# Column sums of the modulation vectors: sixteen or eight small matmuls a section, or a fold on VectorE and one matmul

## The chip, the cores and the metric

One core of one Trainium2 chip. The time is the device time of one execution in microseconds; lower is better. TensorE's clock has two levels, 1.2 and 2.4 GHz, and the profile gives the granted share of the higher one.

## The reference

Two transformer stacks, each of two layers, run one after the other on 256 tokens of width 1024, all in fp32. Each layer has three sublayers: feed-forward, mixer, feed-forward. The first stack also carries 256 context tokens; its mixers are a gated MLP (gMLP) and an attention. The second stack's mixer is a mixture of attention, a causal convolution and gated linear attention. Every sublayer is modulated by vectors that come from a conditioning vector:

```python
def modulation(cond, w_mod, b_mod):
    m = jax.nn.silu(cond) @ w_mod + b_mod
    return jnp.split(m[..., None, :], N_MOD, axis=-1)

def modulate(x, shift, scale):
    return x * (1.0 + scale) + shift
```

A sublayer needs three sections of 1024 values: shift (section 0), scale (1) and gate (2). In the first stack there are two conditions, one for the tokens and one for the context; in the second there is one.

## The kernel before, in words

The twelve sublayers are numbered 0 to 11: 0 to 5 the first stack (feed-forward, gMLP, feed-forward, feed-forward, attention, feed-forward), 6 to 11 the second (feed-forward, mixer, feed-forward, twice). Sublayers 0 to 4 work on two streams (512 tokens), the others on one (256).

All engines' programs are written out by hand. The weights of the large matmuls arrive in units of 1 MB (two loads of 512 KB on SyncE's queue into wraw). For each unit ScalarE rounds them to the high half wh (line 834, split_next), VectorE takes the low half wl = wraw - wh (line 1243, split_next), and TensorE makes three matmuls for each product: high by high, low by high, high by low. wraw, wh and wl have two slots each. In turn i of a loop VectorE first splits the weights of unit i+1, then does what is hosted in that turn, then evacuates unit i (line 1630 in the first stack; in the second stack take, lines 1573 to 1575, stands ahead of the split and product, line 1583, after it). TensorE waits for the split (wlo_done) and for the evacuation of two units before (pair_free). A unit has 48 matmuls: 512 columns wide with two streams (line 2240), 258 or 256 in the second stack (lines 2415, 2439, 2268, 2717). In the second block's mixers the projection's units stand between small steps; the order of VectorE's steps there is fixed: turned queries and keys, kt_t (line 2031), then unit work for the next sublayer's modulation.

The modulation vectors of a sublayer are computed while the sublayer before it runs: that one hosts them. (Sublayer 5's sections 0 and 1 are hosted by the second group of sublayer 3; those of sublayer 6 by loops in sublayer 5.) A section's weights, 1024 x 1024, come in four loads of 1 MB into the two buffers of mraw, and VectorE multiplies them in four units, mod_unit (line 1216), two products of 128x1024 for each condition, into a row of partial sums [128, 1024] (acc or lnp). Tables say in which turn each unit stands (TWO_MODS, NEXT_MODS, FF_MODS, MIX_MODS) and after which unit of TensorE the section is finished (TWO_COLUMNS, NEXT_COLUMNS, FF_COLUMNS). Each mod_unit raises mod_used, on which the load into the buffer that it read waits, in SyncE's queue.

What is left is the sum over the 128 partitions. TensorE does it: for each block of 128 columns one fp32 matmul, with the block of the partial sums as the stationary operand and a column of ones moving, which gives a column of 128 sums in PSUM. columns (line 2129) does 8 in a row in the second stack; column (line 2140) puts 16, one after each group of three, between a unit's matmuls in the first stack's hosts. mod_end (lines 1228 to 1237) copies the columns to modc. In the mixers the sections end with columns after unit 5, after the scores (ahead of unit 10), and after the last output unit; the VectorE steps that belong to them are modulation(4), modulation(8) and modulation(13). After the last, VectorE goes on to arrive, which adds the mixer's output to x (take_chunk, line 1428) and makes the low half of the next sublayer's input (low_chunk, line 1446), for which TensorE waits.

The gates of the first stack (section 2) are summed in another way (ones as the stationary operand, lines 2148 and 2158).

Of the kernel before, what the change touches and what calls it, by code (L numbers as in the profile page):

```python
# [6 lines left out]
P = 128  # L7
B2 = 6
F32 = mybir.dt.float32
F32R = mybir.dt.float32r  # L10
# [169 lines left out]
def program(nc, ins, out, subs):  # L180
    u_end = subs[-1]["n_unit"] + dict(ffn=33, gmlp=36, attn=10, mix=16)[subs[-1]["kind"]]
    with ExitStack() as ctx:
# [44 lines left out]
        pos = sb("pos", [P, TT], I32)  # L227
        cgh_, cgl_ = sb("cgh", [P, KD * 16], F32R), sb("cgl", [P, KD * 16], F32R)
        cgh, cgl = cgh_[:], cgl_[:]


# [91 lines left out]
        bias_full, bias_used = sem("bias_full"), sem("bias_used")  # L323
        cols_ready, mcol_done = sem("cols_ready"), sem("mcol_done")
        gate_ps, gate_row, gate_taken = sem("gate_ps"), sem("gate_row"), sem("gate_taken")
        pair_free = sem("pair_free")
# [112 lines left out]
        def summed(s, sec, c):  # L439

            if s["i"] == 5 and sec in (0, 1):
                return lnp[:, sec]
            return lnp[:, c] if 0 < s["i"] < 5 and sec == 1 else acc[:, c]

        def two(s):
# [744 lines left out]
        def _(dve):  # L1190
# [11 lines left out]
            def mod_unit(s, sec, q):  # L1202
# [9 lines left out]
                for jj in range(2):  # L1212
                    for c in cs:
# [5 lines left out]
                                                      op0=ALU.mult, op1=ALU.add)  # L1219
                    if jj == 1:  # L1220
                        op.then_inc(mod_used, 1)
                    elif q == 0:
                        op.then_inc(bias_used, 1)
                        dve.wait_ge(bias_used, sec + (3 * s["i"] + 2))
                    else:
                        steps.link(op)

            def mod_end(s, sec, bank=4, at=0):

                dve.wait_ge(cols_ready, sec + (sections(s, 0) + 1))  # L1230
                nc_ = len(conds(s))
                dst = modc[:, s["i"] % 2, bass.ds(sec, 1), 0:nc_, :].rearrange("p a c k -> p (a c k)")
                if s["block"] == 2 and isinstance(sec, int) and sec == 2:
# [275 lines left out]
            def rope_tables():  # L1509
# [18 lines left out]
                dve.wait_ge(rope2_ready, 1)  # L1528

            dve.wait_ge(in_full, 3 * 16)  # L1530
            dve.wait_ge(svec_ready, 1)
# [20 lines left out]
            for s in subs:  # L1552
# [329 lines left out]
                elif s["kind"] == "mix":  # L1882
# [10 lines left out]
                    def modulation(i):  # L1893
                        if i == 5:
                            mod_end(nxt, 0, 6, 480)
                        if i == 12:
                            factors(nxt)
                        for sec, q in mix_mods(i):
                            mod_unit(nxt, sec, q)
# [139 lines left out]
                    split_next(u0 + 9)  # L2039
                    mod_end(nxt, 1, 6, 488)  # L2040
                    MP.wait(dve, "scores", turn)
# [77 lines left out]
        def _(pe):  # L2119
            def parts(w_hi, w_lo, x_hi, x_lo):  # L2120

                return (w_hi, x_hi), (w_lo, x_hi), (w_hi, x_lo)

            def columns(s, sec, bank=4, at=0, start=True):

                pe.wait_ge(mod_used, sec * 4 + (12 * s["i"] + 6))
                for c in conds(s):
                    for k in range(KD):
# [4 lines left out]
            def column(s, sec, n, bank=4):  # L2133

                if n == 0:
                    pe.wait_ge(mod_used, sec * 4 + (12 * s["i"] + 6))
                c, k = divmod(n, KD)
                if c >= len(conds(s)):
# [204 lines left out]
            pe.wait_ge(ident_ready, 2)  # L2343
            pe.wait_ge(svec_ready, 1)
            cs = slice(2, 3) if subs[0]["block"] == 2 else slice(0, 2)
            nc_ = len(conds(subs[0]))
# [30 lines left out]
            for s in subs:  # L2377
# [278 lines left out]
                elif s["kind"] == "mix":  # L2656
# [112 lines left out]
                    MA.wait(pe, "decays", turn)  # L2769
                    columns(nxt, 0, 6, 480)  # L2770
                    taps(5)
# [39 lines left out]
                    pe.wait_ge(mcol_done, sections(nxt, 0) + 1)  # L2811
                    columns(nxt, 1, 6, 488)
                    unit(10)
# [92 lines left out]
```

## Time and profile before

| | us |
|---|---|
| median of three runs | 3125.51 |
| lowest, highest | 3121.47, 3126.77 |
| the profiled execution, first to last instruction (its span) | 3123.3 |
| TensorE busy in it | 3058.2 |
| VectorE busy in it | 2027.8 |
| ScalarE busy in it | 969.5 |
| GpSimd busy in it | 673.8 |

The profiled execution has a span and no time of its own outside it. Of the span, what counts is which engine is waited for at each place. In the profile PE is TensorE, PEld its weight load, DVE VectorE, ACT ScalarE, POOL GpSimd, SP SyncE. Matmuls are pipelined, so that durations of neighbours overlap: read the distance between their starts.

### The profile page before, as it was taken

How to read it: one execution, taken by the hardware profiler on the slowest of the kernel's cores; microseconds unless marked ns; L12 is line 12 of the kernel's file. 1: busy time of each engine (PE TensorE's matmuls, PEld its weight loads, DVE VectorE, ACT ScalarE, POOL GpSimd, SP SyncE). 2: the span in 40 equal slices, each digit the busy share in tenths (PEclk: the TensorE clock that was granted, in tenths of full speed). 3: DMA queues.
4: the chain of work that ended last, by engine and by line, in shares of the span. 5: the costliest groups of instructions: out<-in, count | busy, mean ns of one | idle time of the engine just before them, and what ended most of it. 6: DMA issues, size and time to landing. Idle time of an engine off the chain costs nothing.

```text
span 3123.3 us, 46661 instructions
## 1 busy us (share of the span) xinstructions
PE 3058.2 (98%) x19308; PEld 2721.5 (87%) x19308; DVE 2027.8 (65%) x2134; ACT 969.5 (31%) x1027; POOL 673.8 (22%) x614
## 2 busy tenths in 40 slices
PE   8999999999999999999999899999999999999999
PEld 5888889988888888888888699899989999999999
DVE  5854358767278433785638777586788767768754
ACT  2211232212131121221114343333544333344443
POOL 1210100124013010130101022231372313228120
PEclk9999999999999999999999999999999999999999
DMA  7643335332246332463623287586557869755564
GB/s 263 200 150 87 102 102 187 118 101 80 95 131 202 108 90 99 122 202 108 201 99 122 95 268 244 174 266 229 191 174 230 270 193 271 245 189 185 166 182 156
DMA packets 501668, 522.79 MB, mean 167 GB/s; under 512 B 15732, under 2 KB 433830, under 8 KB 501478
## 3 DMA queue, kind: packets, MB, share of 16 engines
q1 hardware_dynamic: 498536, 513.76, 51.5%
q0 software_dynamic: 2944, 6.32, 1.0%
q8 instruction: 143, 2.34, 0.3%
q14 instruction: 45, 0.37, 0.0%
HBM read 518.97 MB, written 1.05 MB: 166 GB/s over the span
## 4 chain that ended last, share of the span: by engine, by line
PE 88%; DVE 7%; ACT 3%; DMA 1%; issue 1%; POOL 0%; SPq 0%; DVEq 0%; ACTq 0%
PE ps L2240 29%; PE ps L2415 16%; PE ps L2326 15%; PE ps L2439 8%; PE ps L2268 8%; PE ps L2305 2%; DVE wl L1243 2%; ACT wh L834 1%; PE ps L2352 1%; PE ps L2284 1%; PE ps L2685 1%; PE ps L2129 1%; PE ps L2717 1%; DVE acc L1216 1%; PE ps L2545 1%
## 5 line engine op out<-in xcount | busy, mean ns | idle before, releaser
L1243 DVE TENSOR_TENSOR wl<-wraw,wh 128x2048 fp32r<-128x2048 f32 x341 | 834.2, 2447 | 569.3 <-ACT wh L834 564.4
L834 ACT ACTIVATE wh<-wraw 128x2048 fp32r<-128x2048 f32 x341 | 652.7, 1914 | 935.7 <-PE ps L2326 383.7
L2240 PE MATMUL ps<-xh,wh 128*128 128x512 f32 (+1 forms) x1504 | 564.9, 376 | 0.5 <-DVE xl L1295 0.3
L2240 PE MATMUL ps<-xl,wh 128*128 128x512 f32 (+1 forms) x1504 | 552.6, 367 | 0.0
L2240 PE MATMUL ps<-xh,wl 128*128 128x512 f32 (+1 forms) x1504 | 550.9, 366 | 0.0
L2415 PE MATMUL ps<-xh,wh 128*128 128x258 f32 x1408 | 405.7, 288 | 5.4 <-DVE xl L1446 3.7
L674 POOL CAST hh<-ht 128x256 f32 (+1 forms) x176 | 140.4, 798 | 1218.1 <-DVE ht L1630 883.3
L2415 PE MATMUL ps<-xh,wl 128*128 128x258 f32 x1408 | 401.2, 285 | 0.0
L2415 PE MATMUL ps<-xl,wh 128*128 128x258 f32 x1408 | 400.7, 285 | 0.0
L1216 DVE SCALAR_TENSOR_TENSOR acc<-mraw,svec,acc 128x1024 f32<-128x1024 f32 x259 | 342.5, 1342 | 5.7 <-DVE prea L1282 0.4
L2240 PEld LDWEIGHTS ps<-xl,wh 128*128 128x128 f32 x1504 | 282.9, 188 | 50.0
L2240 PEld LDWEIGHTS ps<-xh,wl 128*128 128x128 f32 x1504 | 283.4, 188 | 44.8 <-issue 0.7
L2240 PEld LDWEIGHTS ps<-xh,wh 128*128 128x128 f32 x1504 | 283.3, 188 | 44.4 <-issue 1.2
L2415 PEld LDWEIGHTS ps<-xh,wh 128*128 128x128 f32 x1408 | 269.8, 192 | 8.8 <-DVE wl L1243 3.7
L2415 PEld LDWEIGHTS ps<-xl,wh 128*128 128x128 f32 x1408 | 270.6, 192 | 0.0
L2415 PEld LDWEIGHTS ps<-xh,wl 128*128 128x128 f32 x1408 | 270.4, 192 | 0.0
L936 ACT ACTIVATE sg<-ps 128x512 f32<-128x512 f32 (+1 forms) x88 | 48.0, 546 | 660.0 <-PE ps L2240 626.5
L2268 PE MATMUL ps<-wh,xh 128*128 128x256 f32 x832 | 240.6, 289 | 5.1 <-DVE wl L1243 4.9
L2268 PE MATMUL ps<-wl,xh 128*128 128x256 f32 x832 | 234.4, 282 | 0.0
L2268 PE MATMUL ps<-wh,xl 128*128 128x256 f32 x832 | 234.4, 282 | 0.0
L675 POOL TENSOR_TENSOR hl<-ht,hh 128x256 f32 (+1 forms) x176 | 219.9, 1250 | 29.2 <-POOL hh L674 29.2
L2326 PE MATMUL ps<-wh,hh 128*128 128x512 f32 x520 | 205.2, 395 | 1.5 <-DVE wl L1243 1.5
(438 smaller groups left out, 5478.4 us busy)
## 6 DMA issues: line engine op xcount, KB each, us to landing
wraw<-in_ffn_w_in SPq DMA_DIRECT2D x352, 512.0 KB, 5.2
wraw<-in_ffn_w_out SPq DMA_DIRECT2D x176, 512.0 KB, 4.2
mraw<-in_ada_w SPq DMA_DIRECT2D x72, 1024.0 KB, 6.8
mraw<-in_w_mod SPq DMA_DIRECT2D x64, 1024.0 KB, 6.7
wraw<-in_gmlp_w_in SPq DMA_DIRECT2D x48, 512.0 KB, 4.4
wraw<-in_mix_w_in SPq DMA_DIRECT2D x48, 512.0 KB, 4.8
wraw<-in_gmlp_w_out SPq DMA_DIRECT2D x24, 512.0 KB, 3.8
first_w<-in_w_mod SPq DMA_DIRECT2D x8, 1024.0 KB, 11.6
```

Source lines behind the costliest of these rows:

```text
L674: steps.link(pool.tensor_copy(hh[:, where], ht[:, par, 0:width]))
L675: pool.tensor_tensor(hl[:, where], ht[:, par, 0:width], hh[:, where].bitcast(F32), ALU.subtract)\
L834: act.activation(wh[:, slot], wraw[:, slot], ACT.Copy).then_inc(whi_done, 1)
L936: act.activation(sg[:, pair, 0:W], ps[:, 2 * pair, 0:W], ACT.Silu).then_inc(sg_ready, 1)
L1216: op = dve.scalar_tensor_tensor(out=to, in0=mraw[:, q % 2, jj], scalar=svec[:, v, 2 * q + jj:2 * q + jj + 1], in1=biasrow[:] if q == jj == ...
L1243: dve.tensor_tensor(wl[:, slot], wraw[:, slot], wh[:, slot].bitcast(F32), ALU.subtract)\
L2240: m = pe.matmul(ps[:, bank, 0:width], a, b, start=k == p == 0, stop=k == KD - 1 and p == 2)
L2268: m = pe.matmul(to, a, b, start=k == p == 0, stop=k == KD - 1 and p == 2)
L2305: m = pe.matmul(ps[:, 2 * t + half], a, b, start=False, stop=i == kk == 1 and p == 2, skip_group_check=i == 0)
L2326: m = pe.matmul(ps[:, bank0 + 2 * t + half], a, b, start=start and kk == p == 0, stop=stop and kk == 1 and p == 2, skip_group_check=not st ...
L2415: m = pe.matmul(ps[:, 2 * pair + r, 0:XW], a, b, start=n == p == 0, stop=n == KD - 1 and p == 2)
L2439: m = pe.matmul(ps[:, j, 0:T], a, b, start=i == kk == p == 0, stop=i == KF // 2 - 1 and kk == 1 and p == 2, skip_group_check=i == 5)
```

## The change

Where a section is folded (function folded: sections 0 and 1 of sublayers 1 to 5, all three of 7 to 11), VectorE does most of the sum over partitions itself. After the last product it transposes the partial sums in blocks of 32x32, into the buffer of mraw that it has just used up, and sums over each block's 32 columns; this leaves [128, 32], fold, in which each group of 32 partitions holds its part of all 1024 sums. Only then is mod_used raised. TensorE adds the four groups with one fp32 matmul, 32 columns for each condition, whose stationary operand fold_ident is an identity folded to 32 and repeated four times. mod_end picks the sums with four small copies, one for each quarter of the partitions, in place of one.

```diff
+        with ExitStack() as early:
+            fold = early.enter_context(nc.sbuf_tensor("fold", [P, 2, 32], F32))
+        fold_ident = sb("fold_ident", [P, 4, 32])
...
+        def folded(s, sec):
+            return isinstance(sec, int) and (s["i"] in (1, 2, 3, 4, 5) and sec < 2 or s["i"] in (7, 8, 9, 10, 11))
+        def fold_at(s, sec):
+            return sec if s["i"] == 5 else 0
...
-                    if jj == 1:
+                    if jj == 1 and q == 3 and folded(s, sec):
+                        steps.link(op)
+                        for c in cs:
+                            m = steps.mark(dve.transpose(mraw[:, 1, c], summed(s, sec, c)))
+                        for c in cs:
+                            steps.wait(m - len(cs) + 1 + c)
+                            op = dve.reduce_sum(fold[:, c + fold_at(s, sec)], mraw[:, 1, c].rearrange("p (f j) -> p f j", j=32), axis=AX.X)
+                        op.then_inc(mod_used, 1)
+                    elif jj == 1:
                         op.then_inc(mod_used, 1)
...
+                if folded(s, sec):
+                    for b in range(4):
+                        row = slice(32 * b, 32 * b + 32)
+                        dst = modc[row, s["i"] % 2, sec, 0:nc_]
+                        src = ps[row, bank, at:at + 32 * nc_].rearrange("p (c k b) -> p c k b", c=nc_, b=4)[:, :, :, b]
+                        if sec == 2 and s["kind"] == "ffn":
+                            op = dve.tensor_scalar(dst, src, 0.5, None, ALU.mult)
+                        else:
+                            op = dve.tensor_copy(dst, src)
+                    op.then_inc(mcol_done, 1)
+                    return
...
+            dve.wait_ge(ident_ready, 2)
+            steps.link(dve.reduce_sum(fold_ident[:, 0], ident[:].rearrange("p (b i) -> p i b", b=4), axis=AX.X))
+            dve.tensor_copy(fold_ident[:, 1:4], fold_ident[:, 0:1].broadcast_to([P, 3, 32])).then_inc(fold_ready, 1)
...
+            def sums_of_blocks(s, sec, bank, at, start):
+                w, f = 32 * len(conds(s)), fold_at(s, sec)
+                pe.matmul(ps[:, bank, at:at + w], fold_ident[:].rearrange("p b i -> p (b i)"),
+                          fold[:, f:f + len(conds(s))].rearrange("p c f -> p (c f)"), start=start, stop=True,
+                          skip_group_check=not start).then_inc(cols_ready, 1)
...
             def columns(s, sec, bank=4, at=0, start=True):
                 pe.wait_ge(mod_used, sec * 4 + (12 * s["i"] + 6))
+                if folded(s, sec):
+                    sums_of_blocks(s, sec, bank, at, start)
+                    return
...
             def column(s, sec, n, bank=4):
                 if n == 0:
                     pe.wait_ge(mod_used, sec * 4 + (12 * s["i"] + 6))
+                    if folded(s, sec):
+                        sums_of_blocks(s, sec, bank, 0, True)
+                if folded(s, sec):
+                    return
```

fold lies over cgl, which a mixer uses only before its first fold. In the mixers the place of the sums in PSUM moves from columns 480 and 488 of bank 6 to 448 and 480. Before its first matmul TensorE also waits for fold_ready.

## Rows read from the trace of the kernel before

**Rows 1.** The page: busy time and instructions of each engine; chain by engine

```profile
PE 3058.2 (98%) x19308; PEld 2721.5 (87%) x19308; DVE 2027.8 (65%) x2134; ACT 969.5 (31%) x1027; POOL 673.8 (22%) x614
PE 88%; DVE 7%; ACT 3%; DMA 1%; issue 1%; POOL 0%; SPq 0%; DVEq 0%; ACTq 0%
```

**Rows 2.** Lines 2129, 2140: count, ns min/median/max, first and last start, forms

```profile
L2129 PE MATMUL ps<-ones,acc x288: 164/250/353, 1845.1 to 2921.8; 128*128 128x1 f32 x144
...
L2140 PE MATMUL ps<-ones,lnp x160: 164/210/250, 166.4 to 1569.3; 128*128 128x1 f32 x160
...
L2140 PE MATMUL ps<-ones,acc x128: 164/210/250, 129.7 to 1356.2; 128*128 128x1 f32 x128
```

**Rows 3.** Timeline of TensorE, sublayer 5 and mixer: start, us, engine, line, operands, count

```profile
1845.10 1.84 PE L2129 MATMUL ps<-ones,acc 128*128 128x1 f32 x16
1846.81 0.36 PE L2240 MATMUL ps<-xh,wh 128*128 128x256 f32 x1
...
2315.01 0.56 PE L2823 MATMUL ps<-proj,sc_t 128*128 128x64 f32 x4
```

**Rows 4.** Timeline of TensorE inside a unit of sublayer 0 with columns

```profile
129.44 0.39 PE L2240 MATMUL ps<-xl,wh 128*128 128x512 f32 x1
129.67 0.28 PE L2140 MATMUL ps<-ones,acc 128*128 128x1 f32 x2
...
130.36 0.39 PE L2240 MATMUL ps<-xl,wh 128*128 128x512 f32 x1
```

**Rows 5.** Timeline of ScalarE: it starts as units 5, 6, 7 of sublayer 0 end

```profile
118.19 0.60 ACT L936 ACTIVATE sg<-ps 128x512 f32<-128x512 f32 x1 [8.58 <-PE ps L2240]
...
129.18 0.60 ACT L936 ACTIVATE sg<-ps 128x512 f32<-128x512 f32 x1 [8.58 <-PE ps L2240]
...
143.67 0.60 ACT L936 ACTIVATE sg<-ps 128x512 f32<-128x512 f32 x1 [12.08 <-PE ps L2240]
```

**Rows 6.** Groups of VectorE by line: busy us, mean ns of one, idle before

```profile
L1243 DVE TENSOR_TENSOR wl<-wraw,wh 128x2048 fp32r<-128x2048 f32 x341 | 834.2, 2447 | 569.3 <-ACT wh L834 564.4 <-DVE x L1380 0.7 <-DVE x L1344 0.4
...
L1380 DVE TENSOR_SCALAR x<-x,mv,rstd 128x1024 f32<-128x1024 f32 x20 | 16.6, 874 | 8.3 <-POOL rstd L671 8.3
...
L1931 DVE TENSOR_REDUCE nrm<-om 128x16 f32<-128x1024 f32 x4 | 4.8, 1205 | 0.0
...
L1236 DVE COPY modc<-ps 128x8 f32<-128x8 f32 (+2 forms) x22 | 3.6, 162 | 2.9 <-PE ps L2129 2.6
```

**Rows 7.** Timeline of VectorE in sublayer 0: products of turn 5, next split

```profile
113.62 11.49 DVE L1216 SCALAR_TENSOR_TENSOR acc<-mraw,svec,acc 128x1024 f32<-128x1024 f32 x8
...
125.64 2.28 DVE L1243 TENSOR_TENSOR wl<-wraw,wh 128x2048 fp32r<-128x2048 f32 x1
```

**Rows 8.** Timeline of VectorE in sublayer 2: products of turn 7

```profile
973.85 10.09 DVE L1216 SCALAR_TENSOR_TENSOR lnp<-mraw,svec,lnp 128x1024 f32<-128x1024 f32 x8
```

**Rows 9.** Timeline of VectorE in sublayer 6: turn 8's products; a later split

```profile
2067.33 2.61 DVE L1216 SCALAR_TENSOR_TENSOR acc<-mraw,svec,acc 128x1024 f32<-128x1024 f32 x2
...
2165.64 2.29 DVE L1243 TENSOR_TENSOR wl<-wraw,wh 128x2048 fp32r<-128x2048 f32 x1 [0.84 <-ACT wh L834]
```

**Rows 10.** VectorE's busy time in both mixers, section 0's products to kt_t

```profile
2258.00:2299.50 41.50, 39.60 (x38) 1.00 0.72 242
2814.80:2857.70 42.90, 39.46 (x37) 1.00 0.69 234
```

**Rows 11.** Timeline, first mixer: products of sections 1 and 2; TensorE after columns

```profile
2299.55 3.05 DVE L1216 SCALAR_TENSOR_TENSOR acc<-mraw,svec,acc 128x1024 f32<-128x1024 f32 x2
...
2357.11 5.32 DVE L1216 SCALAR_TENSOR_TENSOR acc<-mraw,svec,acc 128x1024 f32<-128x1024 f32 x4 [0.21 <-DVE prea L1282]
...
2366.53 0.56 PE L2415 MATMUL ps<-xh,wh 128*128 128x258 f32 x1 [1.11 <-DVE xl L1446]
```

**Rows 12.** Busy times, granted clock (sixth) and DMA: unit 10 of both mixers

```profile
2305.30:2312.40 7.10, 7.10 (x49) 7.10 (x50) 6.89 (x15) 0.00 (x0) 6.56 (x7) 0.79 0.80 293
2863.30:2869.10 5.80, 5.80 (x51) 5.80 (x51) 5.58 (x13) 0.00 (x0) 5.35 (x6) 1.00 0.85 307
```

More of the change, by code:

```diff
@@ L227, in program @@
         pos = sb("pos", [P, TT], I32)
-        cgh_, cgl_ = sb("cgh", [P, KD * 16], F32R), sb("cgl", [P, KD * 16], F32R)
+        cgh_ = sb("cgh", [P, KD * 16], F32R)
+        with ExitStack() as early:
+            fold = early.enter_context(nc.sbuf_tensor("fold", [P, 2, 32], F32))
+        cgl_ = sb("cgl", [P, KD * 16], F32R)
         cgh, cgl = cgh_[:], cgl_[:]
+        fold_ident = sb("fold_ident", [P, 4, 32])
         def alias(*shapes):
@@ L324, in program @@
         cols_ready, mcol_done = sem("cols_ready"), sem("mcol_done")
+        fold_ready = sem("fold_ready")
         gate_ps, gate_row, gate_taken = sem("gate_ps"), sem("gate_row"), sem("gate_taken")
@@ L1894, in modulation @@
                         if i == 5:
-                            mod_end(nxt, 0, 6, 480)
+                            mod_end(nxt, 0, 6, 448)
                         if i == 12:
@@ L2039, in _ @@
                     split_next(u0 + 9)
-                    mod_end(nxt, 1, 6, 488)
+                    mod_end(nxt, 1, 6, 480)
                     MP.wait(dve, "scores", turn)
@@ L2344, in _ @@
             pe.wait_ge(svec_ready, 1)
+            pe.wait_ge(fold_ready, 1)
             cs = slice(2, 3) if subs[0]["block"] == 2 else slice(0, 2)
@@ L2769, in _ @@
                     MA.wait(pe, "decays", turn)
-                    columns(nxt, 0, 6, 480)
+                    columns(nxt, 0, 6, 448)
                     taps(5)
@@ L2811, in _ @@
                     pe.wait_ge(mcol_done, sections(nxt, 0) + 1)
-                    columns(nxt, 1, 6, 488)
+                    columns(nxt, 1, 6, 480)
                     unit(10)
```

## The prediction, made before the change was built

> **What bounds the kernel now.** I read the page first, then the lines of the small matmuls, then timelines of VectorE at each place where a section ends. The page [rows 1] shows TensorE busy 98% of the span and 88% of the chain that ended last, VectorE 65% and 7%. Taken alone that says that every instruction taken from TensorE is won. The timelines say otherwise: where modulation is hosted, VectorE is nearly full too, and it is just in time. So each section has to be read at its own place.
>
> The removed work [rows 2]: 288 matmul instructions on line 2140 (128 on acc, 160 on lnp; each fp32 matmul is two) and 288 on line 2129, of which the 48 of sublayer 6 stay. So 144 + 120 = 264 column matmuls go, 25 small ones come (8 sections with two conditions, 2 for sublayer 5, 15 of sublayers 7 to 11).
>
> **What they cost TensorE.** A burst of 16 instructions takes 1.71 us to the next matmul, which comes a little late [rows 3]: 1.78 us a section. Between 512-column matmuls the group of three and one column sum takes 0.92 us [rows 4]; the ordinary pitch is 10.99/48 = 0.229 us, so a column costs 0.233 and a two-condition section 3.7. The units agree: 14.49 us with columns, 10.99 without [rows 5], and 0.2 more in the next unit. The new matmul has no row; four fp32 instructions of 64 columns fill 0.56 us [rows 3], so it costs 0.28 at most, by the columns' own pitch 0.21; I take 0.25. TensorE thus gets 3.45 us free in a two-condition section (3.35 in the gMLP, by the same reading of its units) and 1.53 in a single one. The instructions in the burst are 107 ns apart [rows 3] though they stream one column. The Trainium skill (TensorE: Matmul & The Clock Gate, section Wait — 56ns, not 53.3ns?) puts the floor between small matmuls at about 25 ns; by that rule the removed work would cost a quarter, the 11 single sections below would win 1.3 us less and the 8 double ones 2.7 less, and the sum would be some 36 us worse, a plain loss. The rows decide.
>
> **What VectorE gets.** Per condition one block transpose and one sum of 128x1024, 66 operations in all. The sum has a row, line 1931: 1.21 us [rows 6]. The transpose has none. Nearest below is a one-input operation of that shape, 0.87 (line 1380); above, a pass over 2048 elements, 2.45 (line 1243). I take 1.2, the sum's, which has the same shape and one input. With the two semaphore steps: 2.5 us for one condition, 4.8 for two. Evacuation becomes four copies, three more of at most 0.16 each by line 1236 [rows 6]; pipelined I take 0.25 for the three. The setup of the folded identity runs while the first 1 MB loads are awaited: nothing; without that cover under 1 us. No DMA changes, but the load into the second buffer of mraw waits for the later mod_used, and SyncE's weight loads queue behind it; those weight loads also wait for the split behind the fold, so this is counted there.
>
> **Place by place.** In every loop, weights for unit i+1 are split on VectorE in turn i, 2.3 us, after the products and evacuation of turn i-1. A fold ahead of it is free only while the split still ends before TensorE is done with unit i.
>
> *Sublayer 0.* Products end at 125.1, the split for unit 7 ran 125.6 to 127.9 [rows 7], unit 7 started at 129.2 [rows 5]: 1.3 us of slack against 4.8. Unit 7 starts at 132.9, lasts 11.2 in place of 14.5, ends at 144.2 (was 143.6). The next turns have 6.3, 11.0, 6.4 + 4.8, 6.3 and 11.1 us of products, each with 2.3 of split and 0.65 of evacuation: they make unit 9 wait 1.1, unit 10 wait 3.0 and the unit after 11 wait 1.2, which starts at 193.8 in place of 191.6. **+2.2 us**; all of the gain is eaten.
>
> *Sublayers 1, 2 and the first group of 3.* The first fold comes after one unit of products and fits. The second follows two (973.9 to 983.9 [rows 8]); with the fold, evacuation and split it ends at about 988.1, when TensorE, 3.45 us earlier, is ready at 986.8: 1.3 us of waiting (1.9 in the gMLP, which waits 0.5 there already). -5.2, -5.6, -5.6: **-16.4 us**.
>
> *Sublayer 3, second group* (hosts sublayer 5): a turn has 2.3 + 5.0 + 2.5 + 0.65 = 10.5 us in 11.0, it fits. Two sections, **-3.2 us**.
>
> *Second block's feed-forwards, features* (6 sections). Products end at 2069.9 [rows 9]; fold 2.5, three small operations 0.74, split 2.3: weights at 2075.6. The columns ended at 2075.8, TensorE without them is ready at 2074.3. It waits for VectorE instead: -0.25 each, **-1.5 us**. *Their output units* (3 sections): products end at 2164.8, the next split, which idled 0.84 [rows 9], ends 1.6 us later, 0.6 after it is due: -0.9 each, **-2.7 us**.
>
> *Mixers.* From section 0's last product to kt_t VectorE is busy 39.6 of 41.5 us in the first mixer and 39.5 of 42.9 in the second [rows 10]. In the first, 2.5 of fold and 0.25 of copies arrive whole at the product at 2299.6 [rows 11], after which TensorE waits for kt_t; in the second a 2.4 us wait for ScalarE absorbs all but 1.0. Section 1's fold stands there itself, ahead of the split for unit 10, +2.5, less 0.4 of slack: +4.85 and +3.4. Section 2: products run 2357.1 to 2362.4 [rows 11] and the arrival of the next sublayer's input follows without a gap; TensorE idled 1.1 us after its columns for it. The fold stands in that chain, so the columns' 1.8 us win nothing and 2.5 + 0.25 are lost, twice. **+13.8 us**.
>
> *Clock.* Unit 10 of the first mixer took 7.1 us at a granted 0.79, that of the second 5.8 at 1.00 [rows 12]; a stretch at 1.2 GHz costs some 1.5 us. I count one more in the second mixer, one in sublayer 0, after its longer waits: **+3.1 us**.
>
> Sum: 2.2 - 16.4 - 3.2 - 4.2 + 13.8 + 3.1 = -4.7 us. The sum is against the profiled span, 3123.3 us, 2.2 under the median of 3125.5 and inside the spread of the three runs; applied to the median it gives **3121 us**.
>
> **Bounds.** Counting the folds that stand on the path (4 in sublayer 0, 6 in 1 to 3, 9 in feed-forwards, 6 in mixers), one microsecond more per transpose costs 25 us. With 0.87 the sum is -13, with 2.45 it is +26.
>
> **Rivals.**
> *More slack than I read*: waits that end first (ScalarE's weights, POOL's rsqrt) swallow half of the mixers' 13.8 and the sublayer 0 loss: about 3110. For it, the 1.9 and 3.4 us of idle time [rows 10]; against, these lie before, not after the waits. 0.18.
> *All of TensorE's time is won*: 6 x 3.45 + 2 x 3.35 + 3.2 + 13 x 1.53 = 50.5: 3075. The page speaks for it, rows 7, 9 and 11 against. 0.03.
> *Slower*: the transpose costs a second pass. The place is the same queue, the price 25 us per us; it decides from 1.4 us a transpose (sum zero), and from 1.65 the kernel is over 0.2% slower; at 2.45 it is 3152. Against it, the sum, with one input of the same shape, takes 1.21 [rows 6]. 0.10. The Trainium skill (Vector Engine (DVE) Microarchitecture Reference, section 3.8 The reshape front-end and per-opcode configuration) says that the transpose sustains one element per cycle per lane; no run here shows it yet.
> *Clock*: each new wait over 2.5 us, two in sublayer 0 and six in mixers, some twice, brings a stretch at 1.2 GHz: 8 to 10 x 1.5 in place of 3.1, 3131. For it, a 0.79 stretch stands right where the first mixer's TensorE had waited [rows 12]; against, units that wait for VectorE anyway lose nothing by it. 0.12.
> *The change does not do what it says*: column sums sat in time that TensorE had to spare and folds likewise, 3125. Rows 4 and 5 speak against. 0.05.
>
> **Numbers.** The forecast has 0.52 (its own range 3114 to 3130). A measurement of this kernel can tell about 0.2%, 6.3 us. Faster by more: 0.17 of the forecast, nearly all of the slack case, all of the won case: 0.37. Slower: the transpose and half of the clock case, a little of the forecast: 0.20. The rest, 0.43, is within. Range 3109 to 3134, which leaves out the 50 us win and the upper transposes.
>
> **What would show it.** Line 2240 units of sublayers 1 to 3 at 11.2 us where they had 14.5; a wait of TensorE for wl in sublayer 0 near 129 us of over 3 us, in each feed-forward about 1.2 us after the tenth and eighteenth units, in the mixers before unit 10 of 4 us; low_chunk 2.7 us later at the mixers' ends. Transposes away from 1.2 us, or mixers no longer than before, would make the prediction wrong.

## The result, and the profile after

| | before | after |
|---|---|---|
| median of 4 runs each, us | 3123.78 | 3137.91 |
| lowest, highest, us | 3121.47, 3126.77 | 3137.52, 3139.95 |
| ratio, 95% interval | | 1.0045 (1.0031 to 1.006) |
| span of the profiled execution, us | 3123.3 | 3135.8 |
| mean granted clock in it | 0.993 | 0.987 |

The change makes the kernel 14 us slower. Forecast were 3121 us and at most 3134; slower by over 0.2% had a chance of 0.20.

The page of the changed kernel, busy time of each engine and chain by engine, against [rows 1]:

```profile
PE 3023.2 (96%) x18830; PEld 2677.7 (85%) x18830; DVE 2122.4 (68%) x2277; ACT 971.0 (31%) x1027; POOL 693.3 (22%) x614
PE 71%; DVE 20%; issue 4%; ACT 4%; DMA 1%; POOL 1%; SPq 0%; DVEq 0%; ACTq 0%; POOLq 0%
```

TensorE is busy 35 us less and the span is 12.5 us longer: 47.5 us of waiting were added. The chain says for whom. VectorE held 7% of it and now holds 20%.

The new groups by line (busy us, mean ns of one, idle before), which answer to [rows 6]:

```profile
L1239 DVE TENSOR_REDUCE fold<-mraw 128x32 f32<-128x1024 f32 x33 | 39.2, 1206 | 0.6
L1236 DVE STREAM_TRANSPOSE mraw<-acc 128x1024 f32<-128x1024 f32 x23 | 28.2, 1238 | 0.7
L1261 DVE COPY modc<-ps 32x8 f32<-32x8 f32 (+1 forms) x88 | 14.4, 163 | 1.2
L2162 PE MATMUL ps<-fold,fold_ident 128*128 128x32 f32 (+1 forms) x50 | 8.2, 244 | 6.1 <-DVE fold L1239 6.1
```

The prices were forecast well: a transpose takes 1.24 us where 1.2 was taken, a sum 1.21. So the rival that the transpose costs a second pass is out, by its own condition. The Trainium skill (Vector Engine (DVE) Microarchitecture Reference, section 3.8 The reshape front-end and per-opcode configuration) says that it sustains one element per cycle per lane. The trace shows no cycles; it agrees in that a transpose of 1024 elements per lane takes as long as a sum of as many (1.24 and 1.21 us), so one pass and not two. TensorE's saving has its size too: the units that had 14.49 us [rows 5] take 11.2.

So the loss is a matter of place. The ends of TensorE's weight units can be read in both traces as in [rows 5]. How far each stands behind or ahead of the kernel before, and by how much that changes over a stretch, gives this table:

| stretch | forecast, us | measured, us |
|---|---|---|
| sublayer 0, with its first output unit | +2.2 | +8.3 |
| sublayer 1 | -5.2 | -6.9 |
| sublayer 2 | -5.6 | -1.4 |
| sublayer 3, first group | -5.6 | -1.4 |
| sublayer 3, second group | -3.2 | -3.2 |
| feed-forwards 6, 8, 9 | -4.2 | -5.0 |
| first mixer | +7.6 | +12.2 |
| second mixer | +6.1 | +11.4 |
| clock, one stretch each in sublayer 0 and the second mixer | +3.1 | in the rows above |
| between these | 0 | -1.4 |
| sum | -4.7 | +12.5 |

Where VectorE's turn had room (second group of 3, feed-forwards) the forecast holds within a microsecond. Where it had none, every place but sublayer 1 came out 4 to 6 us worse. The signs that the forecast named came nevertheless: TensorE stands idle 3.4 us for wl in sublayer 0, 1.8 and 1.7 us ahead of unit 10, and 2.4 us longer than before at the mixers' ends. So the named waits were there, and more beside them. Timelines say what is new.

**Sublayer 0.** VectorE after, at the first section's end and at the last turn (start, us, then engine, line, operands, count, idle before):

```profile
125.13 2.37 DVE L1236 STREAM_TRANSPOSE mraw<-acc 128x1024 f32<-128x1024 f32 x2
127.42 2.31 DVE L1239 TENSOR_REDUCE fold<-mraw 128x32 f32<-128x1024 f32 x2
129.64 0.68 DVE L1665 TENSOR_TENSOR ht<-ps,sg 128x512 f32<-128x512 f32 x1
130.24 2.29 DVE L1275 TENSOR_TENSOR wl<-wraw,wh 128x2048 fp32r<-128x2048 f32 x1
...
191.08 0.71 DVE L1261 COPY modc<-ps 32x16 f32<-32x16 f32 x4
195.50 2.29 DVE L1275 TENSOR_TENSOR wl<-wraw,wh 128x2048 fp32r<-128x2048 f32 x1 [3.70 <-ACT wh L847]
```

The first four lines are the forecast to 0.1 us: split at 130.2, where it stood at 125.6 [rows 7]. The last is not in it: at 191.8 VectorE is free and stands 3.7 us, since ScalarE has no weights to round. SyncE's queue after, with 1 MB modulation loads (x2) and then the four loads of the output units:

```profile
176.39 9.47 SPq L513 DMA_DIRECT2D mraw<-in_w_mod  x2
186.25 2.55 SPq L528 DMA_DIRECT2D wraw<-in_ffn_w_out  x4
```

Before, the same two groups:

```profile
167.23 9.85 SPq L500 DMA_DIRECT2D mraw<-in_w_mod  x2
177.46 2.55 SPq L515 DMA_DIRECT2D wraw<-in_ffn_w_out  x4
```

Everything there is 9 us later, and the weights stand in the queue behind a load that waits for VectorE's mod_used.

**Sublayers 2 and 3.** VectorE after, in the turns of the two-unit section end of sublayer 2:

```profile
969.05 0.71 DVE L1261 COPY modc<-ps 32x16 f32<-32x16 f32 x4
969.79 2.29 DVE L1275 TENSOR_TENSOR wl<-wraw,wh 128x2048 fp32r<-128x2048 f32 x1
972.00 11.13 DVE L1229 SCALAR_TENSOR_TENSOR lnp<-mraw,svec,lnp 128x1024 f32<-128x1024 f32 x8
983.17 2.37 DVE L1236 STREAM_TRANSPOSE mraw<-lnp 128x1024 f32<-128x1024 f32 x2
985.47 2.30 DVE L1239 TENSOR_REDUCE fold<-mraw 128x32 f32<-128x1024 f32 x2
987.80 0.69 DVE L1665 TENSOR_TENSOR ht<-ps,sg 128x512 f32<-128x512 f32 x1
988.41 2.28 DVE L1275 TENSOR_TENSOR wl<-wraw,wh 128x2048 fp32r<-128x2048 f32 x1
```

TensorE behind that split:

```profile
987.22 0.39 PE L2289 MATMUL ps<-xl,wh 128*128 128x512 f32 x1
990.74 0.79 PE L2289 MATMUL ps<-xh,wh 128*128 128x512 f32 x1 [3.14 <-DVE wl L1275]
```

The split ends at 990.7 in place of 988.1. The four copies take 0.71 us, 0.55 more than one and not 0.25, and the eight products take 11.13 us where [rows 8] has 10.09. TensorE's row is idle for 3.14 us, and TensorE went on at 1.2 GHz, until 994.1 us.

**Mixers.** GpSimd after, raising to a power for the queries' factors nrm ("the power" from here on), and VectorE beside it:

```profile
2252.84 5.04 POOL L684 TENSOR_TENSOR nrm<-nrm,mhalf 128x16 f32<-128x16 f32 x1 [2.45 <-DVEq L1538]
...
2252.78 2.29 DVE L1275 TENSOR_TENSOR wl<-wraw,wh 128x2048 fp32r<-128x2048 f32 x1
2257.91 1.23 DVE L1974 TENSOR_TENSOR proj<-proj,nrm 128x1024 f32<-128x1024 f32 x1 [2.84 <-POOL nrm L684]
```

The same before:

```profile
2259.87 2.94 POOL L671 TENSOR_TENSOR nrm<-nrm,mhalf 128x16 f32<-128x16 f32 x1 [0.23 <-DVEq L1506]
...
2260.00 2.29 DVE L1243 TENSOR_TENSOR wl<-wraw,wh 128x2048 fp32r<-128x2048 f32 x1 [0.33 <-ACT wh L834]
2262.84 1.23 DVE L1939 TENSOR_TENSOR proj<-proj,nrm 128x1024 f32<-128x1024 f32 x1 [0.55 <-POOL nrm L671]
```

Before, the split waited 0.33 us for ScalarE and so began 0.13 behind the power. After, the fold has made VectorE late, wh is there, and the split begins 0.06 ahead of the power, which then takes 2.1 us more; VectorE's next step needs it and waits 2.84 us in place of 0.55. After, it is so in both mixers; before, the second mixer's power had begun 2.2 us ahead of its split.

Busy times of four stretches after, behind the folds of sections 1 and 2 in both mixers (length, busy PE, PEld, DVE, ACT, POOL, granted clock, DMA):

```profile
2300.00:2311.00 11.00, 8.71 (x51) 8.63 (x52) 10.71 (x21) 0.00 (x0) 10.33 (x8) 0.69 0.59 202
2363.00:2378.00 15.00, 10.37 (x50) 9.75 (x50) 13.81 (x26) 7.21 (x14) 2.18 (x3) 0.66 0.44 141
2866.00:2877.00 11.00, 7.59 (x44) 7.51 (x45) 10.71 (x21) 0.00 (x0) 10.36 (x8) 0.69 0.52 190
2930.00:2944.00 14.00, 9.63 (x44) 9.02 (x45) 13.54 (x26) 7.21 (x14) 2.18 (x3) 0.63 0.27 75
```

TensorE is idle for 2.3 to 4.6 us in each, VectorE for no more than 1.2. A granted 0.69 is 6.8 of 11 us at 1.2 GHz, 0.63 is some 10.2 of 14; the second mixer's unit 10 ran at 1.00 before [rows 12].

### The profile page after: what moved, and what is told of

Read it like the earlier page. It is cut to its first block, busy times and chain, and to the rows that moved or that the text cites. A ratio compares the mean times of both kernels' runs of the same rounds, so it can differ in the third digit from the quotient of the medians.

```text
span 3135.8 us, 45849 instructions
## 1 busy us (share of the span) xinstructions
PE 3023.2 (96%) x18830; PEld 2677.7 (85%) x18830; DVE 2122.4 (68%) x2277; ACT 971.0 (31%) x1027; POOL 693.3 (22%) x614
## 4 chain that ended last, share of the span: by engine, by line
PE 71%; DVE 20%; issue 4%; ACT 4%; DMA 1%; POOL 1%; SPq 0%; DVEq 0%; ACTq 0%; POOLq 0%
PE ps L2289 21%; PE ps L2375 15%; PE ps L2465 14%; PE ps L2489 7%; DVE acc L1229 5%; DVE wl L1275 4%; PE ps L2317 4%; PE ps L2354 3%; DVE lnp L1229 2%; ACT wh L847 2%; DVE mraw L1236 1%; PE ps L2402 1%; PE ps L2333 1%; DVE fold L1239 1%; PE ps L2767 1%
## 5 line engine op out<-in xcount | busy, mean ns | idle before, releaser
L2465 PE MATMUL ps<-xh,wh 128*128 128x258 f32 x1408 | 406.3, 289 | 17.5 <-DVE xl L1478 10.1
L2317 PE MATMUL ps<-wh,xh 128*128 128x256 f32 x832 | 238.7, 287 | 12.5 <-DVE wl L1275 12.2
L688 POOL TENSOR_TENSOR hl<-ht,hh 128x256 f32 (+1 forms) x176 | 233.6, 1327 | 29.2 <-POOL hh L687 29.2
```

Of the source, the lines that this page charges most:

```text
L688: pool.tensor_tensor(hl[:, where], ht[:, par, 0:width], hh[:, where].bitcast(F32), ALU.subtract)\
L2317: m = pe.matmul(to, a, b, start=k == p == 0, stop=k == KD - 1 and p == 2)
L2465: m = pe.matmul(ps[:, 2 * pair + r, 0:XW], a, b, start=n == p == 0, stop=n == KD - 1 and p == 2)
```

## The experiments

Each is timed beside the kernel before on its chip, and the ratio is to that; the change itself stands at 1.0045 in its first run and 1.0042 in its second.

### Where in the kernel: mixers or elsewhere

```diff
 def folded(s, sec):
-    return isinstance(sec, int) and (s["i"] in (1, 2, 3, 4, 5) and sec < 2 or s["i"] in (7, 8, 9, 10, 11))
+    return isinstance(sec, int) and (s["i"] in (1, 2, 3, 4, 5) and sec < 2 or s["i"] in (7, 9, 10))
```

> The change as it is, but the sections that the two mixers host (those of sublayers 8 and 11) are summed by columns again; all else is folded. Theory A (the loss sits where the folds stand in VectorE's queue ahead of work that TensorE waits for, above all in the mixers, where the ends of units moved by +12.2 and +13.0 us): 3113 us, 25 less than the changed kernel. Rival B (the folds slow the whole kernel by what they add to VectorE's load and to memory traffic, evenly over the 33 folds): 6 of 33 folds away, 3133 us. Rival C (the new matmul and the four copies are what is dear): 6 of 25 matmuls away, no more than 4 us less, 3134.

Measured: 3111.2 us, before 3124.4, ratio 0.9955 (0.9938 to 0.9971).

```diff
+    return isinstance(sec, int) and s["i"] in (8, 11)
```

> Only the sections that the mixers host are folded, all others are summed by columns as before the change. Theory A: 25 us over the kernel before, 3149 us, and both mixers as long as in the changed kernel. Rival B: under 5 us over it, 3127.

Measured: 3146.1 us, 1.0069 (1.0052 to 1.0086), 21.7 us over before. Both agree with A and neither with an even spread: the six sections of the mixers cost 22 us, the other 19 win 13. The two sum to +8.5 and not to +14; each has an interval of some 5 us, so that this is within their doubt. By the unit ends the mixers are 9.3 and 10.4 us longer than before here and not as long as in the change (12.2 and 11.4), with the same folds in them, so that this part of A's forecast did not hold; GpSimd's power, below, has more on this.

### The two halves of the change

TensorE's part alone:

```diff
+                if q == 3 and folded(s, sec):
+                    at = fold_at(s, sec)
+                    steps.link(dve.memset(fold[:, at:at + len(cs)], 0.0))
...
-                            m = steps.mark(dve.transpose(mraw[:, 1, c], summed(s, sec, c)))
...
-                            op = dve.reduce_sum(fold[:, c + fold_at(s, sec)], mraw[:, 1, c].rearrange("p (f j) -> p f j", j=32), axis=AX.X)
```

> TensorE's part alone: the small matmul on fold and the four copies are there; in place of the transposes and sums VectorE only sets fold to zero ahead of the fourth unit's products, so the sums over partitions of the folded sections are left out. Theory A (TensorE's saving is real everywhere, and VectorE's added work takes it back): 3083 us, some 41 under the kernel before (50.5 less what the mixers' ends cannot use, four copies and the setting of fold in their chains). Rival C (the new matmul, the copies and the clock cost as much as the columns did): 3110 or more.

Measured: 3081.2 us, 0.9872 (0.9856 to 0.9887): 42.9 us won. This kernel leaves out the sums over partitions, so it shows times alone.

VectorE's part alone:

```diff
-                if folded(s, sec):
+                if False:
                     for b in range(4):
...
-                if folded(s, sec):
-                    sums_of_blocks(s, sec, bank, at, start)
-                    return
```

The same lines go from column.

> VectorE's part alone: transposes and sums are there and raise mod_used, but TensorE still makes all the column sums and mod_end makes one copy; the folds' result is not used. Theory A (the folds cost only where they end after TensorE is ready): 3160 us (3154 to 3168): about 8 in sublayer 0, 4 in sublayers 1 to 3, nothing in the feed-forwards of the second stack, 28 in the mixers, less where columns are hidden behind VectorE. If the two parts simply add (changed kernel = before + VectorE's part + TensorE's part of -45): 3183.

Measured: 3156.7 us, 1.0104 (1.0087 to 1.0121): 32.3 us lost. The halves sum to -11 and together they give +13: with the folds in place, taking the column sums away is worth some 19 us and not 43. That TensorE then waits for VectorE is what the chain says (20% of it in the change, 7% before). Two places had next to nothing to win even without folds. By the unit ends of TensorE's part alone the mixers change by -1.3 and +0.6 us, and in sublayer 0 its 5.2 us are gone (+0.9) with the first output unit.

### GpSimd's power

```diff
                     sum_squares(0)
+                    steps.link(dve.memset(fold[:, 1], 0.0))
+                    steps.link(dve.memset(fold[:, 1], 0.0))
                     split_next(u0 + 5)
```

> The changed kernel with two small settings of an unused half of fold, one after the other, between GpSimd's request for the queries' factors and the split behind it in both mixers, so that GpSimd's power starts ahead of the split. Theory H (that power takes 5.03 us in place of 2.94 when VectorE's two-input split starts just before it, and TensorE's wait for proj follows it): the power back at 2.9 us, TensorE's wait for proj near 2275 us shorter by some 1.8, the kernel 3 to 4 us faster than the changed one, 3134. If the length of the power has another cause: 5.0 again and 3138.

Measured: 3131.4 us, 1.0028 (1.0016 to 1.004); the change in the same batch 3135.9. VectorE and GpSimd in this kernel's first mixer:

```profile
2253.62 2.94 POOL L684 TENSOR_TENSOR nrm<-nrm,mhalf 128x16 f32<-128x16 f32 x1 [2.45 <-DVEq L1538]
...
2253.88 2.29 DVE L1275 TENSOR_TENSOR wl<-wraw,wh 128x2048 fp32r<-128x2048 f32 x1
2256.60 1.22 DVE L1974 TENSOR_TENSOR proj<-proj,nrm 128x1024 f32<-128x1024 f32 x1 [0.42 <-POOL nrm L684]
```

Two operations of 0.09 us that compute nothing put the power ahead of the split, it takes 2.94 us again, and VectorE's wait for it is 0.42. TensorE's wait for proj goes from 1.92 us to 1.19 in the first mixer and from 1.93 to under 0.1 in the second, where 1.8 less were expected. The intervals of the two ratios overlap, so that the 4.5 us by medians need the trace beside them. From a mixer's start to the unit ahead of the scores, four profiles with the long power (the change's two, mixers only, and the weights' loads below) lose 3.6 to 3.8 us to the kernel before in the first mixer and 1.7 in the second; this one loses 1.6 and wins 0.4. So the long power costs 2.1 us in each mixer, as much as it is longer.

Over the whole of the mixers this profile is 4.9 and 2.8 us shorter than the change's in the same batch, but what goes beyond 2.1 isn't shown to come of the power. From the change to the kernel with other loads in sublayer 0 nothing in the mixers differs, the power takes 5.04 us in both, and yet its profile has them 3.0 and 2.6 us shorter, with 27 us at 1.2 GHz in place of 37. Nor do the slow stretches alone account for that: the kernel with mixers only has 41 us of them there and mixers 3.0 and 1.0 us shorter than the change's. So with the same folds a mixer's time differs by up to 3 us between profiles, and no run shows why.

### The clock

```diff
+                    keep_going(0, 8)
                     columns(nxt, 1, 6, 480)
+                    keep_going(0, 8)
...
+                    keep_going(2, 6)
                     columns(nxt, 2, 3)
+                    keep_going(2, 15)
```

> The changed kernel with small matmuls that compute nothing where TensorE waits in the two mixers for folds: 8 before and 8 after the one matmul of section 1, 6 before and 15 after that of section 2, so that it is not idle ahead of its work. No work of VectorE changes. Theory E (stretches at 1.2 GHz behind the long waits are a large part of the mixers' loss): 3130 us, 8 less than the changed kernel, and the granted clock at 2302 and 2367 us back at 1.00. Theory A alone (VectorE's queue sets these places, the clock only makes slow what would wait anyway): 3136 to 3138.

Measured: 3131.4 us, 1.0023 (1.0013 to 1.0032), over 10 runs from 3125 to 3140. The four stretches in its profile, which is that of its slowest run (the program starts 2 us later there, mixers 5 to 7):

```profile
2307.00:2318.00 11.00, 11.00 (x82) 11.00 (x82) 9.55 (x19) 0.00 (x0) 10.27 (x9) 0.84 0.52 191
2369.00:2384.00 15.00, 13.43 (x104) 12.12 (x102) 14.70 (x27) 7.77 (x15) 2.18 (x3) 1.00 0.46 144
2869.00:2880.00 11.00, 11.00 (x92) 10.31 (x92) 10.71 (x20) 0.00 (x0) 10.18 (x10) 1.00 0.35 119
2934.00:2948.00 14.00, 12.41 (x84) 11.23 (x82) 12.51 (x24) 7.24 (x15) 2.18 (x3) 0.88 0.28 77
```

The granted clock is up at all four, at two of them to 1.00 (at the first, 6.8 us at 1.2 GHz remain, begun earlier in the work), and by the unit ends the mixers are 1.7 and 1.8 us shorter than in the change's first profile. The control, the changed kernel once more:

> The changed kernel once more, on this chip, as what the two runs of the last batch are compared with (small matmuls in the mixers' waits; the first output unit's loads ahead): 3138 us. If those two had won nothing and only their chip was faster, this comes out near 3131.

Measured: 3135.9 us, 1.0042 (1.0029 to 1.0056). So the fillers win some 6 us by the ratios (0.0019 of 3124, with about 5 us of doubt; the intervals overlap) and 3.5 by the traces. The granted clock rises as E expected, though at 2307 us not to 1.00. What it costs is not settled: the mixers here, 10.6 and 9.6 us over before, lie within what profiles with the same folds and no fillers show (9.3 to 12.3 and 8.8 to 12.0). That the clock is a part of the mixers' loss is likely and not shown; where it is low, it is so behind waits that VectorE's folds made.

### The weights' loads of sublayer 0

The first output unit's two loads are issued ahead of the last load of modulation weights, in SyncE's program:

```diff
-                for sec, q in two_mods(s, n, TWO_LOADS):
+                late = two_mods(s, n, TWO_LOADS)
+                held = late[1:] if s["i"] == 0 else []
+                for sec, q in late[:len(late) - len(held)]:
...
+                    for idx in range(n):
+                        load(u0 + idx, u0 + idx, src(idx), by_column)
+                        if idx == 0:
+                            for sec, q in held:
+                                load_mod(subs[1], sec, q, sec * 4 + (12 * 1 + q + 1))
```

> The changed kernel, but in sublayer 0 the loads of the first output unit's weights are issued ahead of the last load of modulation weights, which in SyncE's queue waits for mod_used. Theory F (the 5.6 us that the unit ends of sublayer 0 slip at the first output unit come from those weights' loads, held in SyncE's queue behind that wait): VectorE's wait for wh at 195 us is gone, 3134 us, 4 less. If VectorE's queue alone set it: no change, 3138.

Measured: 3130.8 us, 1.002 (1.0009 to 1.0031), about 7 us less than the change by ratios, again over a wide 3123 to 3138. Its SyncE queue and VectorE at that place:

```profile
174.91 0.37 SPq L513 DMA_DIRECT2D mraw<-in_w_mod  x1
175.32 0.94 SPq L528 DMA_DIRECT2D wraw<-in_ffn_w_out  x2
184.01 0.38 SPq L513 DMA_DIRECT2D mraw<-in_w_mod  x1
...
190.33 2.29 DVE L1287 TENSOR_TENSOR wl<-wraw,wh 128x2048 fp32r<-128x2048 f32 x1
```

The loads leave at 175.3 in place of 186.3, the split follows the copies with no wait, and the unit that had slipped 5.6 us slips 1.3: 4.3 us at this place, where 4 were expected. F holds. The rest of the 7 is not of this place; this profile's mixers are shorter too, as said above.

### The fold put off by a turn

Two things are changed at once from here on. The eight sections hosted by sublayer 0 and by the mixers are left to the column sums, so that 17 of 25 are folded. Of these the folds of six in the first stack and nine in the second run in the next turn, behind the split (in the second stack behind the product), and raise mod_used there:

```diff
-            return isinstance(sec, int) and (s["i"] in (1, 2, 3, 4, 5) and sec < 2 or s["i"] in (7, 8, 9, 10, 11))
+            return isinstance(sec, int) and (s["i"] in (2, 3, 4, 5) and sec < 2 or s["i"] in (7, 9, 10))
...
-                        steps.link(op)
-                        for c in cs:
...
+                        if s["i"] in DEFERRED:
+                            pending.append((s, sec, steps.mark(op)))
+                        else:
+                            fold_section(s, sec, steps.mark(op))
...
                                 split_next(u0 + i)
+                                fold_pending()
```

> The fold is taken out of the place ahead of the next split: the transposes and sums of a section run in the turn after its last product, behind that turn's split of weights (in the second stack's feed-forwards behind its product, a turn without products), and mod_used is raised there. Folded are the sections of sublayers 2, 3, 4 (in this way), 7, 9, 10 (in this way) and 5 (as in the change); those of sublayer 1 and of the two that mixers host are summed by columns. Theory A (what costs is only that the fold stands ahead of a split that TensorE waits for): 3086 us: 3 x 6.9 in sublayers 1 to 3, 3.2 in the second group of 3, 9 x 1.6 in feed-forwards of the second stack, all under the kernel before. Rival D (VectorE's work as a whole paces these turns, and a fold put off only moves the wait by a turn): about 3111, as with the mixers' sections unfolded and the rest as in the change.

Measured: 3112.0 us, 0.9966 (0.9954 to 0.9979). That is D's number and not D's reason. At the start of the second stack's first feed-forward the unit ends stand 26.8 us ahead of the kernel before, where TensorE's part alone stands at 30.9; behind it the gain runs down to 14. There SyncE's queue shows what VectorE's does not:

```profile
2033.28 6.63 SPq L529 DMA_DIRECT2D wraw<-in_ffn_w_in  x4
2047.58 0.37 SPq L514 DMA_DIRECT2D mraw<-in_ada_w  x1
2047.99 6.32 SPq L529 DMA_DIRECT2D wraw<-in_ffn_w_in  x4
```

The load of modulation weights leaves with the end of the fold at 2047.5, eight microseconds after the last load of weights, and the four loads behind it go out as a bunch.

```diff
-DEFERRED = (2, 3, 4, 7, 9, 10)
+DEFERRED = (2, 3, 4)
```

> As the kernel with folds put off, but in the second stack's feed-forwards the folds stand where the change has them; only those of sublayers 2, 3 and 4 run behind the next split. Sublayer 1 and the mixers' sections are summed by columns. From the unit ends of two runs: 26.8 us won up to the second stack (kernel with folds put off) and 5.8 in it (changed kernel without the mixers' folds), 32 under the kernel before: 3092 us. If the gain of the first stack was one profile's luck: 3105 or more.

Measured: 3092.4 us, 0.9902 (0.9887 to 0.9917), as expected. It is 17 us faster by the ratios than the change without the mixers' sections. By the unit ends 8 of these come from the sections of sublayer 0, now summed by columns, and the rest from the place of the folds: sublayers 1 to 3 stand at -7.9, -6.1 and -6.6 us where the change had -6.9, -1.4 and -1.4. VectorE in the turn behind the two-unit products of sublayer 2:

```profile
962.90 11.13 DVE L1246 SCALAR_TENSOR_TENSOR lnp<-mraw,svec,lnp 128x1024 f32<-128x1024 f32 x8
974.07 0.69 DVE L1680 TENSOR_TENSOR ht<-ps,sg 128x512 f32<-128x512 f32 x1
974.68 2.28 DVE L1289 TENSOR_TENSOR wl<-wraw,wh 128x2048 fp32r<-128x2048 f32 x1
976.87 2.37 DVE L1222 STREAM_TRANSPOSE mraw<-lnp 128x1024 f32<-128x1024 f32 x2
979.16 2.31 DVE L1225 TENSOR_REDUCE fold<-mraw 128x32 f32<-128x1024 f32 x2
```

The same work in another order: the split ends 14.1 us after the products begin, where it took 18.7 in the change, and in that turn TensorE waits for nothing.

The second stack's folds again a turn later, now with a scratch that no load waits for:

```diff
+                        if s["i"] in OWN:
+                            op.then_inc(mod_used, 1)
+                            pending.append((s, sec, None))
...
+                    steps.link(dve.transpose(acc[:, 1], acc[:, 0]))
+                    dve.reduce_sum(fold[:, 0], acc[:, 1].rearrange("p (f j) -> p f j", j=32), axis=AX.X).then_inc(fold_done, 1)
```

> As the last, but the folds of the second stack's feed-forwards run in the turn after the products, with a scratch of their own (the unused second row of acc) in place of mraw, so that mod_used is raised by the last product as before the change and only TensorE waits for the fold. Theory G (the put-off folds lost there because mod_used came late, which held a load of modulation weights and behind it four loads of weights in SyncE's queue): TensorE wins 1.56 us in each of the 9 sections: 27 + 14 = 41 under the kernel before, 3083 us. Rival D (VectorE is too full in these turns wherever the fold stands): 3092 to 3110, with TensorE waiting for wl in the turn behind the fold.

Measured: 3098.8 us, 0.9915 (0.9901 to 0.9928): better than 3112, not the 3083 of G, and 6 us behind the last one, whose second stack has its folds in place. Of SyncE's bunch nothing is left; TensorE's timeline after unit 10 shows another wait:

```profile
2047.34 0.28 PE L2493 MATMUL ps<-xl,wh 128*128 128x258 f32 x1
2049.18 0.41 PE L2187 MATMUL ps<-fold,fold_ident 128*128 128x32 f32 x2 [1.56 <-DVE fold L1223]
```

The small matmul stood where the columns had stood, and the fold ends later than they could begin.

```diff
-FF_COLUMNS = (10, 18)
+FF_COLUMNS = (11, 19)
```

> The kernel with folds of the second stack in the turn after the products and a scratch of their own, with the matmul on fold and mod_end one unit later there (after the 12th and 20th unit in place of the 11th and 19th). In its predecessor's trace TensorE came to that matmul 1.85 us before the fold's end, in each of the 6 places: the fold of turn 9 ends later than unit 10 on TensorE. Theory I (nothing else holds these sections): that wait is gone, each of the 6 sections wins 1.5 us against the unfolded kernel in place of losing 0.25, 10 less than the predecessor's 3099 and 6 less than the 3092 of the kernel with the folds left in place there: 3087 us. Rival D (VectorE too full): TensorE waits for wl instead, 3092 or more.

Measured: **3084.9 us**, 0.9877 (0.9861 to 0.9894), 38 us under the kernel before in its batch, and the unit ends show -1.5 in each of the six sections. Theory I holds, and the kernel is faster than the change and than the kernel before.

## Why the prediction was wrong, point by point

By the unit ends the forecast missed 17 us: 10 in the mixers, 8 in sublayers 2 and 3, 6 in sublayer 0, less some 7 elsewhere (3 of them the clock's own term, which the measured rows hold). It named the places and the engine rightly. What failed are its waits: it put at nothing what a late VectorE does to SyncE's queue, to GpSimd beside it and to the turn that follows.

- **What bounds the kernel: right.** The page's 98% of TensorE was not to be trusted, and VectorE is just in time where modulation is hosted. TensorE's part alone wins 43 us (50.5 by rows), the folds take it and more. It also rules out the reading by which the removed work costs a quarter.
- **TensorE's prices: right.** 3.45, 3.35 and 1.53 a section; in TensorE's part alone a two-condition section wins 3.2 to 3.4 us with its unit, and a single one 1.56 to 1.66.
- **VectorE's prices: right for the fold, small for the copies.** Four copies take 0.71 us where one took 0.16: 0.55 more and not 0.25.
- **Sublayer 0: +8.3 and not +2.2.** The step that failed is the sentence that no DMA changes and that SyncE's weight loads "also wait for the split behind the fold, so this is counted there". The loads of the first output unit do not: they wait in the queue behind a load that waits for mod_used of a later unit. 4.3 us of it came back when only their order was changed. What is left, 4.0, holds two stretches at 1.2 GHz of 3.4 us each, where the clock's term had one for 1.5.
- **Sublayers 2 and 3: -1.4 and not -5.6, twice.** The sum was made for a turn alone. The backlog of the first fold, products that ran 1.0 us longer than their row and the copies put the split at 990.7 and not 988.1; the wait for it, 3.1 us and not 1.3, was followed by a stretch at 1.2 GHz (3.4 us long, some 1.6 us lost). That sublayer 1 came out right by 1.7 the other way is luck: it waited 1.4 of the forecast 1.9, and no slow stretch followed.
- **Mixers: +23.6 and not +13.8.** The steps were named rightly (fold and copies ahead of kt_t, fold ahead of unit 10's split, fold ahead of the arrival), two things were missing. The idle 0.33 us of the split before was not spare time: it kept GpSimd's power ahead. The 2.4 us wait for ScalarE, which the forecast let absorb the fold in the second mixer, stood on the same path as the power: VectorE waited 2.8 us there for GpSimd. The experiment gives this 2.1 us in each mixer, 4.2 of the 9.8. The other 5.6 go with the stretches at 1.2 GHz, of which the clock's term had one in the second mixer (1.5). That is argued and not shown: the granted clock is low there and fillers raise it, but with the same folds and the same long power the mixers came out at 18.0 us in one profile (27 us at 1.2 GHz) and at 19.7 in another (41 us), and the fillers' run at 20.2, within that spread. A small slip of the sum stands beside it: the second mixer's 3.4 would be 3.1 by its own terms (1.0 + 2.5 - 0.4).
- **Rivals.** Of the forecast's rivals the clock one (3131 us) was nearest, and it named the new waits over 2.5 us as what brings the slow stretches; it had 0.12. It is half of the truth: the held loads and the power are in no rival. More slack than read (0.18) was the wrong way about. The transpose is out.
- **The numbers.** With the cases of both signs so near each other, one more cost for each full place, of late work that meets something else, would have moved the sum over zero. The range left them out.

What stays open: the profile of the kernel before cannot tell why the eight products take 10.1 us there and 11.1 after; they overlap with other work of GpSimd, and no run took that away. The folds that sublayer 0 hosts weren't tried behind its splits, nor the mixers' folds in another place. What the mixers' 5.6 us are made of is open too, and why that part differs by 3 us between profiles of the same mixers.

## What to carry to other kernels

Work that is moved from a full engine to one that is just in time must go behind the step that the full engine waits for, and the semaphore that it raises must be followed through every queue that waits on it: here 25 sections folded ahead of the splits cost 14 us, and 17 folded behind them win 38, with a buffer and a consumer's place to suit. These are not the same folds. Of the 52 us between the two kernels 30 to 36 come of leaving the eight sections with no room to the columns (28 by runs for the six in the mixers, 22 by unit ends, and 8 for the two in sublayer 0), and 16 to 21 of moving the others: by the rows of the table above these 17 win 18 us where the change has them. So the first question is which places have room, the second where in the turn the work stands. Ask of each place what the late engine now runs beside; an idle third of a microsecond may be what keeps two operations in their order. A forecast that sums a turn alone misses what the turn before left over.

## What the runs showed of the hardware that was not expected

- GpSimd's power on 128x16 took 2.94 us when it began 0.13 or 0.26 us ahead of VectorE's two-input split, and 5.04 when the split began 0.06 us ahead. The split had 2.23 us left, and that and the power make 5.17. The Trainium skill (SBUF — State Buffer, section SBUF: two separate sides) says that GpSimd and a VectorE operation with two inputs in SBUF share a port pair, that the one that starts first has it for its whole instruction, and that the other blocks. The trace agrees for the power behind the split. It does not for the split behind the power: that took its usual 2.29 us beside a power of 2.94, in both mixers of the run with the power first.
- In the changed kernel TensorE's row is idle for 3.1 us or more seven times behind the first 60 us (3.1 to 5.6 us). At each a stretch at 1.2 GHz began, from 2.1 us before the wait's end to 1.3 us behind it. Of four waits of 2.33 us two had such a stretch (at 895.0 and 1666.6 us) and two had none (455.8, 1281.7). Such stretches are 80 us in all there, 44 in the kernel before and 35 in the best one. Matmuls that compute nothing, in four places of the mixers, raised the granted clock at all four (from 0.63 to 0.69 to between 0.84 and 1.00).
- The same 48 matmuls of 512 columns take 10.98 us in some units and 11.20 in others, in runs of ten units or so and not in the same ones of each execution; two profiles of like code can differ by 2 us for this alone.
- In the kernel with folds put off, from 2027 to 2073 us, weight loads of 512 KB that went out in pairs took 3.9 to 6.5 us from issue to landing, and the four behind the held load 6.5 to 9.1 us.
